# The triangular inverse of a chunked recurrence: moving 32 instead of 64 columns at each level, with a row mask in the addition

## The chip, the cores and the metric

The kernel runs on one core of one Trainium2 chip, everything in fp32. The metric is the device time of one execution in microseconds (us). The kernel before was timed three times.

## What is computed

The program is a whole two-block model: x goes through a Fourier-mixing layer and a recurrent layer (each followed by a mixture of experts) and then through two layers of a second block. The change is in the recurrent layer only, in its scan over time, of which there are two, one forward and one backward:

```python
def wkv_scan(r, decay, k, v, a_vec, b_vec, s0, reverse):
    def step(s, inp):
        r_t, w_t, k_t, v_t, a_t, b_t = inp
        sa = jnp.einsum('bhvk,bhk->bhv', s, a_t)
        s = s * w_t[:, :, None, :] + sa[..., None] * b_t[:, :, None, :] + v_t[..., None] * k_t[:, :, None, :]
        return s, jnp.einsum('bhvk,bhk->bhv', s, r_t)
```

There are 16 heads of 64 values; the scan first goes over 256 context positions (their outputs are not needed), then over 512 image positions.

## The kernel before, in words

The scan is cut into chunks of 64 positions (CH): 4 chunks of context and 8 of the image, 12 steps. In each step (`units`) two units are done together, one of each direction; unit u has its tiles in `scr` for direction 0 and in `ring` for direction 1. Within a chunk the recurrence is solved by a 64x64 triangular inverse for each of the 16 heads. Heads are packed in pairs on the 128 partitions: head 2j on rows 0 to 63, head 2j + 1 on rows 64 to 127 (`rows(q)`), so the tiles XI (the inverse built so far), XT (its transpose), GT and the masks' products NM have 128 rows and 8 x 64 columns.

The inverse is built in LEVELS = 6 doublings. Level 0 is the identity plus the neighbours' entries (L1411). At levels l = 1 to 5 blocks of 2^l are joined to blocks of 2^(l+1), by XI = XI + XI N_l XI, where N_l holds only the entries that join two neighbouring blocks:

1. PE, G (L1479): for each head, NM[l] (64x64) as weights, XT as the moving side, 64 columns. The eight matmuls of a group g of four j are one PSUM bank; two groups per unit. An fp32 matmul is two records in the trace, so a unit's G at one level is 32 records, and both units' 64.
2. ACT (L1329): copies G to GT, 256 columns for each group.
3. PE, P (L1490): GT as weights, XI as the moving side, 64 columns; again 32 records for a unit.
4. DVE (L1421): XI = P + XI, 256 columns per group; then (L1426, not at level 5) two transposes of 256 columns make the new XT, for which G of the next level waits.

The order on PE within a level is G(scr), G(ring), P(scr), P(ring). After P of level 1 come 16 transposes of v (V, L1498), which ACT copies out in eight pieces (L1334) before it copies G of level 2; after P of level 2 come 32 transposes (T, L1504). On DVE a level is four operations for scr, then four for ring; at levels 3 to 5 work for the next step (L1375, L1385 to L1391) is queued between them. Before level 1, ACT copies the product of the step's operands (PE, L1467) out of PSUM and POOL multiplies it with the level masks (L1285), two multiplications of some 1.3 us for each level; G of a level waits for its own. After level 5 PE goes on with Q (L1518, L1519), the output (L1528, L1546), S (L1537) and the state (L1557), and ACT and DVE with their copies.

All engines' orders are written out by hand; semaphores stand only where a value is needed. `pairs`, `each` and `rows` are the helpers for the shapes; MD is a table with two 64-column masks for each direction, loaded once by ACT's DMA (L1303) at the start of the scan.

Of the kernel before, what the change touches and what calls it, by code (L numbers as in the profile page):

```python
# [25 lines left out]
P = 128  # L26
# [13 lines left out]
LEVELS = 6  # L40
# [95 lines left out]
def build(nc, a, out, table):  # L136
# [3 lines left out]
    with ctx:  # L140
# [1093 lines left out]
        BKT = [take_scr(NE, CH), held(2, 1024, NE, CH)]  # L1234
        SV = [take_scr(NE, CH), held(4, 0, NE, CH)]
        ZS = [take_scr(8, CH) for _ in range(2)]
        MD = take_scr(2, 128)
        LM = take_scr(2, LEVELS * CH)
        RST = take_scr(512)
        PT = take_scr(4, 8)  # L1240
# [21 lines left out]

        def pairs(t):
            return t[:, 0:256].rearrange("p (j c) -> p j c", c=CH)

        def chunk_streams(d, img):

# [24 lines left out]
        def wkv_scalar(act):  # L1292
# [19 lines left out]
            for n, pair in enumerate(steps):  # L1312
                for u, d, c, img, first in pair:
                    for b4 in range(4):
                        t = tile(act, f"A{u}.{b4}").rearrange("p (h c) -> p h c", c=128)
                        g, q = divmod(b4, 2)
                        if n and later(act, f"nm{u - 2}.{LEVELS - 1}"):
                            act.wait_ge(*at(f"nm{u - 2}.{LEVELS - 1}"))
                        did(A_, act.activation(odd(SC[d][rows(1 - q), 8 * g:8 * g + 8, :], 1)[:, :, 0:CH],
                                               t[rows(1 - q), :, 0:CH], ACT.Copy).then_inc(scalar_done, 1))  # L1320
                        did(A_, act.activation(odd(SC[d][rows(q), 8 * g:8 * g + 8, :], 0)[:, :, 0:CH],  # L1321
                                               t[rows(q), :, 0:CH], ACT.Copy).then_inc(scalar_done, 1), f"nb{u}.{b4}")
                        if not img:
                            marks[f"free.A{u}.{b4}"] = (A_, count[A_])
                for l in range(1, LEVELS):
                    for u, d, c, img, first in pair:
                        for g in range(2):
                            t = tile(act, f"G{u}.{l}.{g}")
                            did(A_, act.activation(GT[d][:, 4 * g:4 * g + 4, :], pairs(t), ACT.Copy).then_inc(scalar_done, 1), f"free.G{u}.{l}.{g}")  # L1329
                    for u, d, c, img, first in pair if l == 1 else ():  # L1330
                        for g in range(2):
                            t = tile(act, f"V{u}.{g}")[0:64, :].rearrange("p (j q c) -> p j q c", q=2, c=CH)
                            for q in range(2):
                                did(A_, act.activation(odd(SV[d][rows(q), 8 * g:8 * g + 8, :], q), t[:, :, q, :], ACT.Copy).then_inc(scalar_done, 1))  # L1334
                            marks[f"free.V{u}.{g}"] = (A_, count[A_])
                    for u, d, c, img, first in pair if l == 2 else ():
                        for q in range(2):
                            t = tile(act, f"T{u}.{q}")
                            did(A_, act.activation(odd(BKT[d], q), t.rearrange("p (h c) -> p h c", c=CH), ACT.Copy).then_inc(scalar_done, 1), f"free.T{u}.{q}")
                    if n + 1 < len(steps) and l >= 4:  # L1340
                        exps(*steps[n + 1][l - 4])
                for u, d, c, img, first in pair:
                    for g in range(2):
                        t = tile(act, f"Q{u}.{g}")
                        did(A_, act.activation(QB[d][:, 4 * g:4 * g + 4, :], pairs(t), ACT.Copy).then_inc(scalar_done, 1), f"free.Q{u}.{g}")
                for u, d, c, img, first in pair:
                    for g in range(2):
                        t = pairs(tile(act, f"S{u}.{g}"))
                        for q in range(2):
                            did(A_, act.activation(odd(SV[d][rows(1 - q), 8 * g:8 * g + 8, :], q), t[rows(1 - q)], ACT.Copy).then_inc(scalar_done, 1))  # L1350
                        marks[f"free.S{u}.{g}"] = (A_, count[A_])

        def wkv_vector(dve):
# [44 lines left out]
            for n, pair in enumerate(steps):  # L1398
# [17 lines left out]
                for l in range(1, LEVELS):  # L1416
                    for u, d, c, img, first in pair:
                        for g in range(2):
                            t = pairs(tile(dve, f"P{u}.{l}.{g}"))
                            x = XI[d][:, 4 * g:4 * g + 4, :]  # L1420
                            did(V, dve.tensor_tensor(x, t, x, ALU.add).then_inc(vector_done, 1), f"xi{u}.{l}.{g}")  # L1421
                            marks[f"free.P{u}.{l}.{g}"] = (V, count[V])
                        if l < LEVELS - 1:
                            dve.wait_ge(*own(dve, V))
                            for g in range(2):
                                did(V, dve.transpose(flat(XT[d][:, 4 * g:4 * g + 4, :]),  # L1426
                                                     flat(XI[d][:, 4 * g:4 * g + 4, :])).then_inc(vector_done, 1), f"xt{u}.{l}.{g}")
                    if n + 1 < len(steps):
                        if l >= 4:
                            tildes(*steps[n + 1][l - 4])  # L1430
                        if l in (3, 4):
                            scan(*steps[n + 1][l - 3])
# [17 lines left out]
        def wkv_tensor(pe):  # L1450
            def each(g):

                return [(j, q, slice((j % 4) * CH, (j % 4) * CH + CH)) for j in range(4 * g, 4 * g + 4) for q in range(2)]

            for pair in units():
                for u, d, c, img, first in pair:
                    bk, ar = BK[d], AR[(u // 2) % 2][d]
# [12 lines left out]
                for l in range(1, LEVELS):  # L1470
                    for u, d, c, img, first in pair:
                        if later(pe, f"nm{u}.{l}"):
                            pe.wait_ge(*at(f"nm{u}.{l}"))
                        for g in range(2):
                            b = bank(pe, f"G{u}.{l}.{g}")
                            if later(pe, f"xt{u}.{l - 1}.{g}"):
                                pe.wait_ge(*at(f"xt{u}.{l - 1}.{g}"))
                            for j, q, o in each(g):
                                ins = pe.matmul(b[rows(q), o], NM[d][l][rows(q), j, :], XT[d][rows(q), j, :],  # L1479
                                                start=True, stop=True)  # L1480
                            did(T_, ins.then_inc(tensor_done, 1), f"G{u}.{l}.{g}")
                    for u, d, c, img, first in pair:
                        for g in range(2):
                            b = bank(pe, f"P{u}.{l}.{g}")
                            if later(pe, f"free.G{u}.{l}.{g}"):
                                pe.wait_ge(*at(f"free.G{u}.{l}.{g}"))
                            if later(pe, f"xi{u}.{l - 1}.{g}"):
                                pe.wait_ge(*at(f"xi{u}.{l - 1}.{g}"))
                            for j, q, o in each(g):
                                ins = pe.matmul(b[rows(q), o], GT[d][rows(q), j, :], XI[d][rows(q), j, :],  # L1490
                                                start=True, stop=True)
                            did(T_, ins.then_inc(tensor_done, 1), f"P{u}.{l}.{g}")
                    for u, d, c, img, first in pair if l == 1 else ():
                        for g in range(2):
                            b = bank(pe, f"V{u}.{g}")
                            for j in range(4):
                                o = (4 * g + j) * CH
                                ins = pe.transpose(b[0:64, j * P:j * P + P], LD[:, d, 1, o:o + CH], ident[:, :])  # L1498
                            did(T_, ins.then_inc(tensor_done, 1), f"V{u}.{g}")
                    for u, d, c, img, first in pair if l == 2 else ():  # L1500
                        for q in range(2):
                            b = bank(pe, f"T{u}.{q}")
                            for j in range(8):
                                ins = pe.transpose(b[:, j * CH:j * CH + CH], BK[d][rows(q), j, :, :], ident[rows(q), rows(q)])  # L1504
                            did(T_, ins.then_inc(tensor_done, 1), f"T{u}.{q}")
# [1195 lines left out]
def constants():  # L2701
# [22 lines left out]
    md, lm = [], []  # L2724
    for d in range(2):
        strict, incl = (s < t, s <= t) if d == 0 else (s > t, s >= t)
        md.append(np.tile(np.concatenate([strict, incl], 1), (2, 1)))
        for l in range(LEVELS):
            lo, hi = (s >> l, t >> l) if d == 0 else (t >> l, s >> l)
            lm.append(np.tile((lo % 2 == 0) & (hi == lo + 1), (2, 1)))  # L2730
# [74 lines left out]
```

## Time and profile before

| | us |
|---|---|
| median of 3 runs | 4351.8 |
| lowest and highest | 4349.01 and 4355.48 |
| the profiled execution, its own time | 4349.7 |
| its span, first to last instruction | 4347.9 |
| mean granted clock of TensorE in the span | 0.933 |
| matmul busy time (PE) | 3772.8 (87%) |
| VectorE, ScalarE, GpSimd busy | 1400.4, 1036.2, 270.1 |
| the scan, from its first level-1 matmul to its end | 559 (1498.2 to 2057.3 us) |

The profile names instructions by line of the kernel. PE is TensorE's matmuls, PEld its weight loads (which overlap the matmuls), DVE is VectorE, ACT ScalarE, POOL GpSimd. The busy time of PE is a union of overlapping matmuls whose ends are modelled, so the time that a run of matmuls takes is read from start to start. In the rows "64*64" is the part of the array that a matmul uses (rows * columns), "64x64" the moving side (partitions x elements). PEclk is the clock that was granted to TensorE as a share of full speed: 1.0 is 2.4 GHz and 0.5 is 1.2 GHz.

### The profile page before, as it was taken

What the parts mean: (1) busy time and instruction counts of PE and PEld (TensorE: products, weight loads), DVE (VectorE), ACT (ScalarE), POOL (GpSimd) and SP (SyncE); (2) the same over time, 40 slices, a digit from 0 to 9 for tenths busy, and PEclk for the clock granted to TensorE, in tenths of its full rate; (3) what the DMA queues carried; (4) which work ended last, traced back from release to release, by engine and by line L of the source; (5) the groups of instructions that cost most, each with busy time, mean ns of one, the idle gap of its engine ahead of it and who ended that gap; (6) DMA issues with size and microseconds to landing.
All of it is one profiled execution on the core that took longest, in us unless ns stands there. A gap on an engine that the chain in (4) does not pass through costs nothing.

```text
span 4347.9 us, 63440 instructions
## 1 busy us (share of the span) xinstructions
PE 3772.8 (87%) x28402; PEld 2309.3 (53%) x28402; DVE 1400.4 (32%) x2400; ACT 1036.2 (24%) x2049; POOL 270.1 (6%) x248
## 2 busy tenths in 40 slices
PE   7989999999789788888787787789689998968998
PEld 3556344334345488887353232335358874535886
DVE  2123000001562256666320000244433334344343
ACT  3021110111341254444210001123122322212231
POOL 0000000000000234333100000000000000000000
PEclk9988999999799899999989999989799999979999
DMA  8345988992233423322349999411023221102320
GB/s 284 104 148 184 347 307 310 364 337 99 87 118 119 119 51 68 83 62 75 132 175 376 385 376 387 147 60 48 27 68 97 93 71 60 55 30 68 97 88 29
DMA packets 526735, 666.87 MB, mean 153 GB/s; under 512 B 156168, under 2 KB 294664, under 8 KB 526464
## 3 DMA queue, kind: packets, MB, share of 16 engines
q1 hardware_dynamic: 505040, 627.89, 42.4%
q10 hardware_dynamic: 17808, 22.29, 1.6%
q0 software_dynamic: 3616, 12.65, 0.8%
q8 instruction: 223, 3.65, 0.3%
q14 instruction: 48, 0.39, 0.0%
HBM read 631.31 MB, written 31.46 MB: 152 GB/s over the span
## 4 chain that ended last, share of the span: by engine, by line
PE 73%; DVE 9%; ACT 5%; DMA 5%; SPq 4%; issue 1%; POOL 1%; ACTq 1%; DVEq 0%; POOLq 0%
PE ps L604 11%; PE ps L467 8%; PE ps L609 4%; DMA ring<-in_moe_wu 4%; SPq L2497 4%; PE ps L797 3%; PE ps L2362 3%; PE ps L2363 3%; PE ps L2364 3%; PE ps L2378 3%; PE ps L2379 3%; PE ps L2377 3%; PE ps L770 3%; PE ps L2086 3%; PE ps L1479 2%; PE ps L1490 2%
## 5 line engine op out<-in xcount | busy, mean ns | idle before, releaser
L604 PE MATMUL ps<-ring,H 128*64 128x512 f32 x2048 | 494.8, 601 | 52.1 <-DMA ring<-in_moe_wu 39.2
L706 DVE TENSOR_TENSOR scr<-ps,scr 128x512 f32<-128x512 f32 x32 | 22.1, 691 | 965.6 <-PE ps L609 516.9
L604 PEld LDWEIGHTS ps<-ring,H 128*64 128x64 f32 x2048 | 148.4, 137 | 342.5 <-issue 251.2
L604 PE MATMUL ps<-ring,scr 128*64 128x512 f32 x1024 | 248.2, 599 | 39.9 <-DMA ring<-in_moe_wd 38.5
L467 PE MATMUL ps<-scr,ring 128*128 128x512 f32 (+1 forms) x640 | 255.8, 563 | 26.9 <-DVE scr L2312 20.9
L2362 PE MATMUL ps<-scr_rounded,ring_rounded 128*128 128x512 f32 x512 | 203.9, 398 | 29.7 <-ACT scr_rounded L2400 29.7
L2431 DVE TENSOR_TENSOR ring_rounded<-ring,scr_rounded 128x2048 fp32r<-128x2048 f32 x64 | 146.7, 2292 | 227.6 <-ACT scr_rounded L2397 227.6
L467 PEld LDWEIGHTS ps<-scr,ring 128*128 128x128 f32 x640 | 124.0, 195 | 160.0 <-issue 130.7
L2363 PE MATMUL ps<-H_rounded,scr_rounded 128*128 128x512 f32 x512 | 204.0, 398 | 0.0
L2364 PE MATMUL ps<-scr_rounded 128*128 128x512 f32 x512 | 203.8, 398 | 0.0
L2379 PE MATMUL ps<-scr_rounded 128*128 128x512 f32 x512 | 202.5, 395 | 0.0
L2377 PE MATMUL ps<-scr_rounded,ring_rounded 128*128 128x512 f32 x512 | 201.8, 394 | 0.0
L2397 ACT ACTIVATE scr_rounded<-ring 128x2048 fp32r<-128x2048 f32 x64 | 122.1, 1907 | 264.3 <-PE ps L2379 246.4
L604 PEld LDWEIGHTS ps<-ring,scr 128*64 128x64 f32 x1024 | 73.0, 136 | 188.7 <-issue 125.1
L1479 PE MATMUL ps<-scr 64*64 64x64 f32 x1920 | 79.8, 239 | 61.0 <-POOL scr L1285 55.0
L797 PE MATMUL ps<-scr 128*128 128x512 f32 (+1 forms) x320 | 125.9, 556 | 4.2 <-ACT scr L680 2.9
L2362 PEld LDWEIGHTS ps<-scr_rounded,ring_rounded 128*128 128x128 f32 x512 | 97.2, 190 | 55.3 <-DVE H_rounded L2436 31.3
L770 PE MATMUL ps<-scr 128*128 128x256 f32 x512 | 121.5, 390 | 4.0 <-DVE scr L877 4.0
L609 PE MATMUL ps<-ring,H 128*32 128x256 f32 x2048 | 123.8, 382 | 0.0
L1285 POOL TENSOR_TENSOR scr<-scr 128x512 f32<-128x512 f32 x72 | 95.0, 1320 | 332.3 <-ACT scr L1321 332.3
L318 ACT ACTIVATE H<-X 128x512 f32<-128x512 f32 (+1 forms) x56 | 36.5, 659 | 326.9 <-DVE X L485 167.7
L2086 PE MATMUL ps<-H,ring 128*128 128x512 f32 x256 | 110.4, 593 | 3.0 <-DVE scr L2039 3.0
(401 smaller groups left out, 6206.8 us busy)
## 6 DMA issues: line engine op xcount, KB each, us to landing
ring<-in_moe_wg SPq DMA_DIRECT2D x128, 1024.0 KB, 9.5
ring<-in_moe_wu SPq DMA_DIRECT2D x128, 1024.0 KB, 8.7
ring<-in_moe_wd SPq DMA_DIRECT2D x128, 1024.0 KB, 10.1
ring<-in_mlp_w SPq DMA_DIRECT2D x64, 1024.0 KB, 5.3
ring<-in_ada_w SPq DMA_DIRECT2D x48, 1024.0 KB, 7.6
ring<-in_w_in SPq DMA_DIRECT2D x14, 1024.0 KB, 5.2
ring<-in_w_out SPq DMA_DIRECT2D x8, 1024.0 KB, 5.1
st_kka<-scr ACTq DMA_DIRECT2D x16, 384.0 KB, 3.5
```

Of the source, the lines that this page charges most:

```text
L467: ins = pe.matmul(b[:, 0:sn], w[:, k, (m % 2) * P:(m % 2) * P + P], rhs(k, s0, sn), start=k == 0, stop=k == kt - 1)
L604: ins = pe.matmul(bx[64 * n:64 * n + 64, :], stat_x(k), w[:, k % 4, :], start=k == 0, stop=k == KT - 1)
L609: ins = pe.matmul(bc[32 * n:32 * n + 32, 0:256], stat_c(k), w[:, k % 4, o:o + 256], start=k == 0, stop=k == KT - 1)
L770: ins = pe.matmul(b[:, 0:256], HT[:, tt, k * P:k * P + P], GM[:, tt, :], start=tt == 0, stop=tt == 3)
L797: ins = pe.matmul(b[:, 0:sn], ys[:, j, m * P:m * P + P], sm[:, j, :], start=j == 0, stop=j == nj - 1)
L2086: ins = pe.matmul(b, w[:, k, (m % 2) * P:(m % 2) * P + P], H[:, k, 0:TX], start=k == 0, stop=k == KT - 1)
L2362: pe.matmul(b, low[:, k, o], hh, start=k == 0, stop=False)
L2363: pe.matmul(b, high[:, k, o], hl, start=False, stop=False)
L2364: ins = pe.matmul(b, high[:, k, o], hh, start=False, stop=k == KT - 1)
L2377: pe.matmul(banks[m], low[:, k, o], hh, start=f == 0, stop=False)
L2379: ins = pe.matmul(banks[m], high[:, k, o], hh, start=False, stop=f == 15)
L2497: did(f"slot{i % NSLOT}", sp.dma_start(dst, src.rearrange("(k p) c -> p k c", p=min(P, rows))).then_inc(sems[f"slot{i % NSLOT}"], 16), "w. ...
```

## The change

At level l the product XI N_l XI has entries only where a row belongs to a block of one parity and a column to a block of the other. The change moves only the columns of that parity: 32 of 64, as 32 / 2^l blocks of 2^l.

- G streams 32 columns of XT (`half_of(XT, ..., d)`) in place of 64, P 32 columns of XI (`half_of(XI, ..., 1 - d)`). The weights of both are the same 64x64 as before, and the number of matmuls, their order, their banks and all waits too.
- ACT's copy takes 128 columns in place of 256 and writes them in blocks into every second block of GT. The other blocks of GT keep what an earlier level or step left there; the rows of P that come of them are not meant to count.
- DVE's addition takes 128 columns in place of 256, reads and writes XI in blocks, and multiplies P by a column of MD (a value per row, 1 for the rows of the right parity and 0 for the others) first: a scalar_tensor_tensor with a scalar operand in SBUF in the place of a tensor_tensor.
- MD gets six columns more for each direction, its one load too.
- The transposes of XI stay at 256 columns. No instruction is added, removed or moved on any queue.

```diff
@@ -1234,7 +1234,7 @@
-        MD = take_scr(2, 128)
+        MD = take_scr(2, 128 + LEVELS)
@@ -1262,6 +1262,13 @@
+        def blocks(t, l, n):
+
+            return t.rearrange("p j (b two s) -> p j b two s", two=2, s=2 ** l)[:, :, :, n, :]
+
+        def half_pairs(t, l):
+            return t[:, 0:128].rearrange("p (j b s) -> p j b s", j=4, s=2 ** l)
@@ -1326,7 +1333,7 @@
                             t = tile(act, f"G{u}.{l}.{g}")
-                            did(A_, act.activation(GT[d][:, 4 * g:4 * g + 4, :], pairs(t), ACT.Copy).then_inc(scalar_done, 1), f"free.G{u}.{l}.{g}")
+                            did(A_, act.activation(blocks(GT[d][:, 4 * g:4 * g + 4, :], l, d), half_pairs(t, l), ACT.Copy).then_inc(scalar_done, 1), f"free.G{u}.{l}.{g}")
@@ -1416,9 +1423,9 @@
-                            t = pairs(tile(dve, f"P{u}.{l}.{g}"))
-                            x = XI[d][:, 4 * g:4 * g + 4, :]
-                            did(V, dve.tensor_tensor(x, t, x, ALU.add).then_inc(vector_done, 1), f"xi{u}.{l}.{g}")
+                            t = half_pairs(tile(dve, f"P{u}.{l}.{g}"), l)
+                            x = blocks(XI[d][:, 4 * g:4 * g + 4, :], l, 1 - d)
+                            did(V, dve.scalar_tensor_tensor(x, t, MD[:, d, 128 + l:129 + l], x, ALU.mult, ALU.add).then_inc(vector_done, 1), f"xi{u}.{l}.{g}")
@@ -1452,6 +1459,12 @@
+            def each_half(g):
+                return [(j, q, slice((j % 4) * 32, (j % 4) * 32 + 32)) for j in range(4 * g, 4 * g + 4) for q in range(2)]
+
+            def half_of(t, q, j, l, n):
+                return t[rows(q), j, :].rearrange("p (b two s) -> p b two s", two=2, s=2 ** l)[:, :, n, :]
@@ -1475,8 +1488,8 @@
-                            for j, q, o in each(g):
-                                ins = pe.matmul(b[rows(q), o], NM[d][l][rows(q), j, :], XT[d][rows(q), j, :],
+                            for j, q, o in each_half(g):
+                                ins = pe.matmul(b[rows(q), o], NM[d][l][rows(q), j, :], half_of(XT[d], q, j, l, d),
                                                 start=True, stop=True)
@@ -1486,8 +1499,8 @@
-                            for j, q, o in each(g):
-                                ins = pe.matmul(b[rows(q), o], GT[d][rows(q), j, :], XI[d][rows(q), j, :],
+                            for j, q, o in each_half(g):
+                                ins = pe.matmul(b[rows(q), o], GT[d][rows(q), j, :], half_of(XI[d], q, j, l, 1 - d),
                                                 start=True, stop=True)
@@ -2724,7 +2737,8 @@
-        md.append(np.tile(np.concatenate([strict, incl], 1), (2, 1)))
+        even = [(np.arange(64)[:, None] >> l) % 2 == d for l in range(LEVELS)]
+        md.append(np.tile(np.concatenate([strict, incl] + even, 1), (2, 1)))
```


## Rows read from the trace of the kernel before

**Rows 1.** The page's part 4, the chain that ended last by engine.

```profile
PE 73%; DVE 9%; ACT 5%; DMA 5%; SPq 4%; issue 1%; POOL 1%; ACTq 1%; DVEq 0%; POOLq 0%
```

**Rows 2.** Busy time by stretch: us, PE, PEld, DVE, ACT, POOL, PEclk, DMA share, GB/s. Scan; level 1's matmuls; after.

```profile
1498.20:2057.30 559.10, 484.95 (x13056) 465.95 (x13056) 355.44 (x770) 280.53 (x748) 212.42 (x165) 0.94 0.30 68
1775.80:1779.10 3.30, 3.30 (x64) 3.30 (x66) 1.15 (x2) 1.15 (x3) 3.30 (x3) 0.51 0.00 0
1779.20:1802.80 23.60, 22.30 (x653) 21.37 (x651) 16.60 (x39) 11.99 (x31) 10.47 (x9) 1.00 0.62 136
```

**Rows 3.** Chain that ended last, 1440 to 2090 us: start us, us, what.

```profile
1501.88 2.24 PE ps L1490 x64
...
1774.02 1.68 POOL scr L1285
1775.74 3.57 PE ps L1479 x64
1779.31 1.87 PE ps L1490 x64
...
2021.54 1.86 PE ps L1490 x64
```

**Rows 4.** Timeline of one step, 1779 to 1801 us: start us, us, engine, line, op, tiles, xcount [idle before].

```profile
1781.11 1.94 PE L1498 MATMUL ps<-ident,H 128*64 128x128 f32 x16
...
1785.50 1.15 PE L1490 MATMUL ps<-scr 64*64 64x64 f32 x32 [0.45 <-ACT scr L1329]
...
1790.99 1.10 PE L1490 MATMUL ps<-scr 64*64 64x64 f32 x32
...
1794.04 0.77 DVE L1426 STREAM_TRANSPOSE ring<-ring 128x256 f32<-128x256 f32 x2
...
1794.63 1.15 PE L1479 MATMUL ps<-ring 64*64 64x64 f32 x32 [0.30 <-DVE ring L1426]
...
1795.59 1.13 PE L1490 MATMUL ps<-scr 64*64 64x64 f32 x32
...
1800.20 1.01 PE L1490 MATMUL ps<-scr 64*64 64x64 f32 x28
```

**Rows 5.** Durations by line (ns min/median/max): level matmuls' weight loads, and L410's.

```profile
L1490 PEld LDWEIGHTS ps<-scr x1920: 129/135/224, 1501.6 to 2044.0; 64*64 64x64 f32 x192
...
L410 PEld LDWEIGHTS ps<-vec,scr x192: 186/192/338, 22.8 to 364.8; 128*128 128x128 f32 x192
```

**Rows 6.** Timeline of PE at 351 us, line 410 at the full clock.

```profile
351.55 0.61 PE L410 MATMUL ps<-vec,scr 128*128 128x2 f32 x4
```

**Rows 7.** Groups by form, whole span: xcount | busy us, mean ns | idle before.

```profile
L706 DVE TENSOR_TENSOR scr<-ps,scr 128x512 f32<-128x512 f32 x32 | 22.1, 691 | 965.6 <-PE ps L609 516.9 <-PE ps L604 448.7
...
L487 DVE SCALAR_TENSOR_TENSOR X<-ps,ada,X 128x256 f32<-128x256 f32 x16 | 7.7, 484 | 29.0 <-PE ps L467 21.6 <-PE ps L797 7.5
...
L1883 ACT ACTIVATE scr<-ps 128x128 f32<-128x128 f32 x12 | 3.3, 277 | 6.9 <-PE ps L1816 6.9
```

**Rows 8.** Groups by form, 1440 to 2080 us, the lines that the change touches.

```profile
L1490 PE MATMUL ps<-scr 64*64 64x64 f32 x1920 | 71.5, 226 | 5.8 <-ACT scr L1329 5.4 <-issue 0.4
...
L1421 DVE TENSOR_TENSOR scr<-ps,scr 128x256 f32<-128x256 f32 x120 | 49.6, 421 | 115.4 <-PE ps L1490 113.4
...
L1329 ACT ACTIVATE scr<-ps 128x256 f32<-128x256 f32 x120 | 43.8, 391 | 105.6 <-PE ps L1479 103.4
```

**Rows 9.** Timeline of PE: matmuls of 64 rows, of 6 rows, then of 128 rows.

```profile
1137.66 21.26 PE L958 MATMUL ps<-scr,ring 64*128 64x512 f32 x32 [1.83 <-ACT scr L1125]
...
3070.14 10.57 PE L2097 MATMUL ps<-H 6*128 6x512 f32 x12 [8.62 <-DVE H L2229]
...
3081.40 1.97 PE L2109 MATMUL ps<-ident,scr 128*128 128x128 f32 x8
```

**Rows 10.** Busy time by stretch, columns as in rows 2: the first two of rows 9.

```profile
1137.40:1157.80 20.40, 20.08 (x30) 10.01 (x31) 6.19 (x11) 11.27 (x22) 3.59 (x6) 0.50 0.65 250
3070.20:3080.60 10.40, 10.40 (x14) 4.04 (x14) 0.00 (x0) 2.98 (x5) 0.00 (x0) 0.50 0.00 0
```


## The prediction

> **What bounds the kernel now.** I first read the chain of waits for the whole span: 73% of it is PE and 9% DVE [rows 1], so time comes off where PE works or waits for DVE. The scan takes 559.1 us of the 4347.9 [rows 2]; nothing outside it is touched. Then the chain inside the scan [rows 3]. A step begins when POOL has made the masks' products, and the next rows are all PE: the 64 records of G at level 1 take 3.57 us, those of P 1.87 us. The same kind of matmul at two speeds: 56 ns a record, then 29. The rows of stretches [rows 2] say why: over the first the granted clock is 0.51 (1.2 GHz), over everything from P to the end of level 5 it is 1.00 (2.4 GHz). The clock has fallen while PE waited for POOL, and it comes back in the middle of level 1, after about one G. The twelve P rows of level 1 run from 2.24 us (first) to 1.86 (last), mean 2.16 [rows 3]: the clock is back for most of each.
>
> The timeline of one step [rows 4] shows the rest. Level 1 ends in V at 1781.11. At level 2 P(scr) waits 0.45 us for ACT, which is still copying V; such waits are 5.4 us in all, 0.45 for each of the 12 steps [rows 8]. At levels 3 to 5 P(scr) starts at 1790.99, 1795.59 and 1800.20, every 4.6 us, while four groups of 0.93 us are 3.7 us. The rest is DVE: G(ring) waits 0.30 us for the transpose that began at 1794.04. So two intervals of a step hang on a loop PE, DVE, PE; the others are PE's own pace.
>
> **The change, part by part.**
>
> *PE's pace at 2.4 GHz: no change.* 32 moving columns in place of 64 halve what is streamed. The question is whether the stream sets the 29 ns a record. Line 410 streams 2 columns against weights of 128 columns: four records in 0.61 us, of which the last one's own 0.251 is latency, so 0.12 us each [rows 6]. Two columns cannot cost that; the weight load does. A load of 128 columns lasts 186 ns at the least, one of 64 columns 129 [rows 5]: 57 ns for 64 columns. The level's matmuls use two corners of the array at once (head 2j, head 2j + 1), so 57 ns of loading on each corner is 28.5 ns a record, what we see. The weights stay 64 columns, hence 0. Bounds: 0, and a halving to 15 ns a record if the stream set the pace (a rival below); I take 0, since [rows 5, 6] are about the load itself. The Trainium skill (TensorE: Matmul & The Clock Gate, LDWEIGHTS) says that a load takes its columns / 1.2 ns, whatever the rows: 53 ns here; the trace agrees. Its section on the back-to-back issue gap has a floor of about 25 ns start to start however few columns are streamed; by it alone a group would go from 0.93 to 0.80 us, and the 20 groups of a step would give back at most 2.6 us. The two-column matmuls [rows 6] speak for the load.
>
> *The clock at level 1: it comes back later.* What raised it was G of level 1. In 1.2 GHz a pair of records takes 115 ns (2 x 57.5), and each corner streams in 107 of them (64 columns at two cycles each), nearly without pause. That the clock does not look at matmuls in flight alone is shown elsewhere [rows 9, 10]: matmuls of 64 rows run for 21.26 us, and of 6 rows for 10.57 us, back to back, PE busy throughout, and the clock stays at 0.50 for the whole time. After the change each corner streams in 53 of 115 ns, so G of level 1 comes to look like those 64-row matmuls rather than like G of today. I therefore expect G and P of level 1 to pass at 1.2 GHz, and the clock to rise in V, 16 transposes with all 128 rows and 128 moving columns. Costs per step: P takes 64 x 57.5 ns = 3.68 us for a mean of 2.16, **+1.5**. V takes at 1.2 GHz 16 x 0.22 = 3.5 us (eight of that shape are 1.97 us including latency [rows 9]) for 1.94, so between 0 and +1.6; since G needed its 3.6 us to raise the clock, I take **+1.3**.
>
> *ACT.* 128 elements of PSUM cost 277 ns, 256 cost 391 [rows 7, 8]: -0.11 us each. Only one copy is on the path, that which P(scr) of level 2 awaits. With V slower, ACT's copies of V finish behind it and well before G of level 2 has run, so the whole wait goes: **-0.45**. At the least it is -0.11.
>
> *DVE.* An addition of 256 elements takes 421 ns and one of 512 takes 691 [rows 7, 8]: 1.05 ns an element, so 128 fewer save 0.13 us. But the scalar operand costs: a scalar_tensor_tensor with one, PSUM and SBUF, takes 484 ns at 256 [rows 7], 0.06 more. Net -0.07 us, 350 ns an addition. In the loop lie the second addition of scr and both of ring (their start-to-start is the part that counts, and it shrinks by less, 0.04 for the first), so about -0.19 us, with -0.03 for P's last record ending 27 ns sooner: -0.215 a loop, two loops a step, **-0.4**. Bounds: 0, if pieces of 2 to 32 elements cost DVE what they save, and -0.4 a loop if the scalar costs nothing. At the other levels DVE is not waited for.
>
> *Free.* MD's load has 12 columns more of 268, once. The transposes, POOL's work, all waits and all orders are the same. If POOL's cover went, G of a level would wait for its mask; it is made levels ahead except at level 1, where POOL, not PE, sets the start, before and after.
>
> Sum per step: 1.5 + 1.3 - 0.45 - 0.4 = +1.95 us, times 12 = **+23 us**. Against the profiled execution's own 4349.7 (span 4347.9 and 1.8 around it) that is 4373; the median of the runs is 2.1 higher, so I predict **4375 us**, 0.5% slower.
>
> **The rivals.**
>
> *A, the above: the clock is late at level 1 and holds afterwards.* 0.55.
>
> *B, it also falls again inside the levels.* At levels 3 to 5 PE will stream half of what it does now, with the gap of the DVE loop still there. Where the clock falls a level of 128 records takes 128 x 57.5 = 7.4 us for 4.6, 2.8 more, or 8.3 us a step until Q (64 columns again) raises it. In every other step that is +50, so 4425; in all steps +100, 4475. For: the stream is as thin as in [rows 9]. Against: now PE pauses in every level too [rows 4], and the clock holds [rows 2]. 0.15.
>
> *C, the clock comes back as before.* The clock would then follow the loads and matmuls as such, of which there are as many as before. Only the gains stand: 12 x (0.43 + 0.11) = -6.5, so 4345, and no measurable difference. Against: [rows 10]. This is also the case in which the change does not do what it says, since PE's work shrinks on paper alone. 0.18.
>
> *D, the other side: the stream sets PE's pace.* The place is every G and P; the price 14.6 ns a record at 2.4 GHz, 28.8 at 1.2. G of level 1 saves 1.8 us, P of level 1 0.9, level 2 1.9 less 0.9 of longer waiting for ACT; each of the two loops holds two groups of 0.47 less and DVE's 0.2, 2.3 together, and the last two groups save 0.9: some 7 us a step, 84 in all, 4268. It decides if a record falls below 29 ns in the timeline. For: two streams of 64 columns are 53 ns on a corner, close to 58, so the present pace can't tell the two apart. Against: [rows 5, 6]. 0.12.
>
> **How the numbers follow.** A measurement of this kernel tells 0.2%, 8.7 us, from no change. A and B are slower: 0.70. C is within it for 0.14, and with a cheaper DVE operand beyond it for 0.04; with D, faster has 0.16. The range goes from C's time, 4343, to B's with half of the steps, 4430; outside it are D and the worse half of B, 0.19. A's own range is 4360 (V's term 0) to 4385.
>
> **What would show it.** In the changed kernel's timeline: 32 records of G or P at 2.4 GHz still in 0.93 us from start to start (if 0.5: D). In the stretches from the start of G at level 1: clock 0.5 through P, and P's 64 records 3.7 us in the chain, not 1.9 (if 1.9: C). V in 3 us or more. No wait of P at level 2 for ACT. P(scr) of levels 3, 4, 5 every 4.4 us with the clock at 1.0; 7.4 and 0.5 would be B. L1421's successor at 350 ns and ACT's copy at 277. The prediction is wrong if the scan, 559 us now, is shorter than 555 or longer than 635.

## The result, and the profile after

| | before | after |
|---|---|---|
| median of 4 runs, us | 4353.34 | 4425.72 |
| lowest and highest | 4349.01 and 4355.48 | 4417.92 and 4431.71 |
| ratio of the times | | 1.0167, interval 1.0144 to 1.0189 |
| profiled execution: span, us | 4347.9 | 4429.9 |
| mean granted clock | 0.933 | 0.908 |

The change makes the kernel 72 us slower, where 23 were forecast. The scan's stretches of time in the kernel after (columns as in [rows 2]; the scan as a whole, then one step in three pieces, then most of another step):

```profile
1495.40:2133.80 638.40, 577.69 (x12996) 554.74 (x12998) 339.33 (x765) 262.25 (x748) 209.90 (x165) 0.76 0.27 59
1767.90:1778.50 10.60, 10.57 (x146) 9.57 (x146) 4.06 (x10) 3.41 (x10) 10.60 (x9) 0.50 0.02 6
1778.60:1795.30 16.70, 15.27 (x478) 14.83 (x477) 10.88 (x28) 7.70 (x23) 3.02 (x3) 1.00 0.85 188
1795.60:1802.00 6.40, 6.40 (x133) 6.40 (x132) 5.41 (x12) 1.80 (x4) 0.00 (x0) 0.50 0.01 3
1592.20:1636.00 43.80, 43.77 (x769) 42.58 (x771) 19.91 (x48) 13.49 (x38) 13.74 (x11) 0.51 0.30 62
```

The clock over the scan is 0.76, where it was 0.94 [rows 2]. In the step from 1767.90 it is 0.50 through all of level 1 (G, P and V), then 1.00, and 0.50 again from the last P on. Before, it was 1.00 from P of level 1 to the end of level 5. The step from 1592.20 never gets it back before Q. The chain of waits of the same two steps (start, us, what; lines are those of the kernel after: L1492 is G, L1503 P, L1511 V):

```profile
1592.22 3.62 PE ps L1492 x64
1595.85 3.41 PE ps L1503 x64
1599.26 3.55 PE ps L1511 x16
...
1767.93 3.63 PE ps L1492 x64
1771.56 3.41 PE ps L1503 x64
1774.97 3.55 PE ps L1511 x16
1778.52 2.00 PE ps L1492 x64
1780.52 1.87 PE ps L1503 x64
...
1795.55 2.97 PE ps L1503 x58
```

Against [rows 3]: G of level 1 is as long as before (3.63 for 3.57), P 3.41 for a mean of 2.16, V 3.55 for 1.94 [rows 4]. P at full clock is 1.87 for 64 records, to the digit what it was with 64 columns. The waits of PE in the scan (us in total, times, longest), and the groups by shape (busy us, mean ns):

```profile
PE ps L1492 <- issue: 2.8, 3, 1.1
PE ps L1492 <- DVE ring L1433: 2.3, 12, 0.4
PE ps L1503 <- issue: 0.6, 2, 0.4
```

```profile
L1428 DVE SCALAR_TENSOR_TENSOR scr<-ps,scr 128x128 f32<-128x128 f32 x120 | 41.2, 348 | 170.0 <-PE ps L1503 166.4
L1336 ACT ACTIVATE scr<-ps 128x128 f32<-128x128 f32 x120 | 32.4, 286 | 128.0 <-PE ps L1492 127.9
```

Besides POOL's 54.9 us ahead of level 1, these are all. P's wait for ACT (5.4 us before, [rows 8]) is gone, an addition takes 348 ns and a copy 286.

To see where the 12 steps spend their time, I took from the timeline of PE the starts of A (the step's operand products), of G of each level, and of Q (L1518 before), and summed the distances over the steps. "Q to A" runs to the next step's A, so it has 11 terms; "all" is the whole row, from the first A to the last Q. The same sums of the experiments below stand here, in us:

| kernel | A to G1 | level 1 | level 2 | level 3 | level 4 | level 5 | Q to A | all |
|---|---|---|---|---|---|---|---|---|
| before | 118.0 | 91.0 | 73.2 | 50.1 | 56.0 | 51.2 | 119.5 | 559.0 |
| after | 118.0 | 125.2 | 75.1 | 54.7 | 63.5 | 68.4 | 133.5 | 638.4 |
| w_l1 | 118.1 | 93.1 | 73.5 | 53.9 | 61.9 | 69.0 | 136.0 | 605.4 |
| w_l2up | 118.1 | 124.9 | 69.1 | 49.2 | 56.0 | 49.5 | 119.8 | 586.7 |
| w_l3up | 118.1 | 124.3 | 67.7 | 51.5 | 56.2 | 47.5 | 119.6 | 584.8 |
| w32 | 118.1 | 79.6 | 60.0 | 45.0 | 60.5 | 48.6 | 132.0 | 543.7 |
| half_add | 118.1 | 91.2 | 73.2 | 49.4 | 56.4 | 48.6 | 120.0 | 556.9 |
| before_fill | 120.8 | 77.1 | 73.2 | 50.4 | 55.4 | 49.2 | 117.2 | 543.3 |
| after_fill | 120.8 | 84.8 | 68.9 | 49.0 | 65.6 | 71.6 | 135.1 | 595.7 |
| after_fill_lv | 120.8 | 101.0 | 74.1 | 60.4 | 64.1 | 55.0 | 116.8 | 592.1 |
| after_fill_ld | 120.8 | 91.9 | 73.9 | 80.1 | 99.9 | 90.3 | 130.9 | 687.8 |
| half_add_fill | 121.0 | 77.1 | 73.3 | 49.8 | 51.1 | 50.7 | 118.8 | 541.8 |
| w_all_fill | 120.6 | 77.1 | 72.0 | 49.9 | 53.6 | 49.2 | 120.2 | 542.6 |

Each row is one execution. That of after is the longest of its four (4431.71 us), so its scan is 79 us longer than before's where the medians are 72 apart. The kernel w_all, below, has no row, since its profiled execution ran in a slow state, at a clock of 0.553 (6515.73 us), while its other eleven took 4342.51 to 4349.60 us.

After against before: level 1 costs 34.2 us more, and levels 2 to 5 and the stretch behind Q 45.2 more. The first number is in the prediction. The second isn't.

### The profile page after: what moved, and what is told of

Same layout as the page of the kernel before. It is cut to its first block, busy times and chain, and to the rows that moved or that the text cites. A ratio compares the mean times of both kernels' runs of the same rounds, so it can differ in the third digit from the quotient of the medians.

```text
span 4429.9 us, 63440 instructions
## 1 busy us (share of the span) xinstructions
PE 3866.1 (87%) x28402; PEld 2401.2 (54%) x28402; DVE 1387.3 (31%) x2400; ACT 1017.9 (23%) x2049; POOL 267.5 (6%) x248
## 4 chain that ended last, share of the span: by engine, by line
PE 75%; DVE 9%; DMA 5%; ACT 4%; SPq 4%; issue 1%; POOL 1%; ACTq 1%; DVEq 0%; POOLq 0%
PE ps L604 11%; PE ps L467 8%; DMA ring<-in_moe_wu 4%; PE ps L609 4%; SPq L2510 4%; PE ps L1492 3%; PE ps L1503 3%; PE ps L797 3%; PE ps L2377 3%; PE ps L2375 3%; PE ps L2376 3%; PE ps L2391 3%; PE ps L2392 3%; PE ps L2390 3%; PE ps L770 3%; PE ps L2099 2%
## 5 line engine op out<-in xcount | busy, mean ns | idle before, releaser
L1492 PE MATMUL ps<-scr 64*64 64x32 f32 x1920 | 88.2, 251 | 59.1 <-POOL scr L1292 54.9
L2375 PEld LDWEIGHTS ps<-scr_rounded,ring_rounded 128*128 128x128 f32 x512 | 97.2, 190 | 54.9 <-DVE H_rounded L2449 31.3
L1492 PEld LDWEIGHTS ps<-scr 64*64 64x64 f32 x1920 | 81.6, 172 | 66.7 <-POOL scr L1292 57.1
```

The costliest lines, as they stand in the source:

```text
L1492: ins = pe.matmul(b[rows(q), o], NM[d][l][rows(q), j, :], half_of(XT[d], q, j, l, d), start=True, stop=True)
L2375: pe.matmul(b, low[:, k, o], hh, start=k == 0, stop=False)
```

## The experiments

Theory 1 is that the 34 + 45 us are all clock, the granted clock of TensorE: a stream of 32 columns neither raises a fallen clock (level 1) nor holds a raised one (levels 3 to 5). Against it stand other costs of the change (pieces of few elements on ACT and DVE, the row mask), a single late rise with consequences, and pauses of PE. The first four kernels were timed together with the kernel before, which took 4350.81 us there.

**w_all**: everything as in the change, but PE streams all 64 columns. ACT and DVE take their 128 elements out of PSUM in blocks.

```diff
-                            for j, q, o in each_half(g):
-                                ins = pe.matmul(b[rows(q), o], NM[d][l][rows(q), j, :], half_of(XT[d], q, j, l, d),
+                            for j, q, o in (each(g) if l >= 1 else each_half(g)):
+                                ins = pe.matmul(b[rows(q), o], NM[d][l][rows(q), j, :], XT[d][rows(q), j, :] if l >= 1 else half_of(XT[d], q, j, l, d),
```

(P likewise, and `blocks(pairs(t), ...)` for `half_pairs(t, l)` on ACT and DVE. Every level has l >= 1, so all are wide.)

> The change with TensorE left as it was: G and P stream 64 columns again, while ScalarE's copy and VectorE's masked addition take only the 128 elements that the change takes (read from PSUM in blocks). Theory 1 (the time was lost by TensorE's clock, because fewer columns are streamed): the clock comes back in level 1 and holds, mean granted clock 0.93, and only the gains of the shorter copy and addition are left: 4345 to 4349 us. Theory 2 (the short pieces, the scalar operand or the block pattern cost the time): slower than before by tens of us, near 4425, with additions or copies longer than 350 and 280 ns or a clock that falls all the same.

Measured 4345.69, ratio 0.9987 (0.9978 to 0.9996). The whole loss is in PE's stream; the copy and the masked addition at half width gain some 5 us, between 2 and 10.

**w_l2up** and **w_l1**: 32 columns at level 1 alone, and at levels 2 to 5 alone (`each(g) if l >= 2 else each_half(g)`, and `l == 1`).

> The change at level 1 only: 32 columns streamed by G and P of level 1, 64 at levels 2 to 5; the copy and the addition at 128 elements everywhere. Theory 1: level 1 takes 10.3 us a step as in the change (7.6 before), so +33, the rest as before less some 6: about 4379 us. If the loss of the levels 3 to 5 and of Q were carried over from a late level 1, the time stays near 4425.

> The change at levels 2 to 5 only: 64 columns streamed at level 1, 32 at levels 2 to 5; copy and addition at 128 elements everywhere. Theory 1: the clock comes back in level 1 (7.6 us a step), then falls again at level 4 or 5 in most steps; no step stays at 1.2 GHz from level 1 to Q, as two do in the change, so about 4380 us (4370 to 4395). If instead the late rise at level 1 is the cause of the later falls, the clock holds and the time is 4345 to 4350.

Measured 4376.99, ratio 1.0057 (1.0043 to 1.0071), and 4396.42, ratio 1.0099 (1.0086 to 1.0113). The chain at level 1, first of w_l2up (L1493 is G, L1504 P):

```profile
1787.04 3.63 PE ps L1493 x64
1790.67 3.41 PE ps L1504 x64
...
1797.51 2.01 PE ps L1493 x64
```

then of w_l1, with the last P of the step:

```profile
1746.09 3.68 PE ps L1493 x64
1749.77 2.47 PE ps L1504 x64
...
1771.14 2.73 PE ps L1504 x58
```

w_l2up has level 1 of the kernel after (124.9 us) and, behind it, everything of before. In w_l1 the clock comes back within level 1 (93.1 us), yet the clock falls in its levels 3 to 5 and behind Q as it does after (69.0 at level 5 and 136.0 behind Q). The two losses, 26 and 46 us, make 72 together: two costs, each with its own place, and the second doesn't follow from the first. w_l1 came out just above the expected 4395, since the clock fell earlier than I had priced: in one step (the second) before level 3, in another within it.

**w32**: the changed kernel with 32 weight columns as well, so half of each product is left out.

```diff
-                                ins = pe.matmul(b[rows(q), o], NM[d][l][rows(q), j, :], half_of(XT[d], q, j, l, d),
+                                ins = pe.matmul(b[64 * q:64 * q + 32, o], NM[d][l][rows(q), j, 0:32], half_of(XT[d], q, j, l, d),
```

(P likewise. ACT's copy is scaled by 1e-6, and DVE's mask column is another column of MD.)

> G and P with weights of 32 columns and 32 streamed columns. Left out: half of each product, and GT is scaled down to nearly nothing, so XI stays at level 0's value; every instruction is there. If the load of 64 weight columns sets the 58 ns of a pair of records, a pair now takes about 30 ns at 2.4 GHz (32 records in 0.48 us) and the level's streams fill that again, so that the clock comes back in level 1 as before: about 4270 us (4260 to 4290). If a fixed cost of an instruction sets it (25 ns or more), 32 records take 0.8 us or stay at 0.93, and the clock behaves as in the change: 4400 or more.

Measured 4336.36, ratio 0.9962 (0.9947 to 0.9977). PE's timeline:

```profile
1774.42 0.69 PE L1492 MATMUL ps<-scr 64*32 64x32 f32 x32
1774.94 0.68 PE L1492 MATMUL ps<-ring 64*32 64x32 f32 x32
...
1787.52 0.51 PE L1492 MATMUL ps<-scr 64*32 64x32 f32 x21 [1.51 <-DVE scr L1433]
```

32 records now take 0.52 us from start to start, 16 ns each, with the same 32 moving columns that took 29 with 64 weight columns. So it is the weight columns, and with them the load, that set the pace at full clock, as the prediction had it. The clock in level 1 of the same step, G and P, then V, and the longest waits of PE in the scan besides POOL's:

```profile
1768.20:1772.50 4.30, 3.69 (x128) 3.54 (x128) 2.18 (x5) 1.15 (x4) 4.30 (x4) 0.50 0.02 4
1772.60:1774.40 1.80, 1.80 (x18) 1.62 (x16) 1.63 (x6) 1.13 (x3) 1.80 (x2) 1.00 0.00 0
```

```profile
PE ps L1503 <- issue: 15.6, 11, 2.7
PE ps L1492 <- issue: 14.9, 17, 1.9
PE ps L1503 <- ACT scr L1336: 14.8, 18, 1.2
PE ps L1492 <- DVE scr L1433: 8.4, 16, 1.5
```

With loads and streams both halved, the stream is as dense in time as before, and the clock does return inside level 1 (79.6 us in all). But in this step it returns only as V begins, so w32 doesn't separate what the dense stream of G and P does for the rise from what V does. The time missed the expected 4270 because PE, done sooner, now stops more: it waits for DVE (1.51 us in the timeline above) and for ACT, and for 30.5 us in G and P with nothing that the profile shows as its reason ("issue"), where the kernel before had 4.1. That pause is the largest of these and its cause isn't known. The clock falls in levels 4 and 5 and behind Q (60.5, 48.6, 132.0); that it falls for these stops wasn't tested. The Trainium skill (TensorE: Matmul & The Clock Gate, Back-to-back issue gap) gives an issue floor of about 25 ns a matmul for 1 to 64 moving columns. Two matmuls on different corners of the array don't keep to it: 16 ns in the mean here.

The next four kernels, half_add_fill at the end among them, were timed with the kernel before at 4349.06 us.

**half_add**: the kernel before with DVE's addition alone at half width, from P in blocks, without a mask.

```diff
-                            t = pairs(tile(dve, f"P{u}.{l}.{g}"))
-                            x = XI[d][:, 4 * g:4 * g + 4, :]
+                            t = blocks(pairs(tile(dve, f"P{u}.{l}.{g}")), l, 1 - d)
+                            x = blocks(XI[d][:, 4 * g:4 * g + 4, :], l, 1 - d)
```

> The kernel before, with one edit: DVE's addition takes only the 128 elements of the right parity, in blocks, out of P as it stands (64 columns, so no row is wrong and no mask is needed: a tensor_tensor without a scalar operand). PE, ACT and the clock's work are untouched. Theory 1 (DVE's part of the change is worth its terms, and only the stream of PE costs): an addition takes 0.29 us in place of 0.42; the two loops of a step that hang on DVE give back 0.25 to 0.4 us each, 12 steps, so -6 to -10 us: 4341 to 4345 for 4350.8, ratio 0.998 to 0.9986. Rival (pieces of 2 elements cost DVE what it saves, or the loop isn't DVE's): 4350, ratio 1.000.

Measured 4347.95, ratio 0.9995 (0.9987 to 1.0004): no difference that can be told, though the loop did shorten. PE's waits, a row of the timeline and the stretch around it:

```profile
PE ps L1482 <- issue: 4.2, 7, 0.9
PE ps L1493 <- issue: 4.1, 5, 1.2
```

```profile
1790.74 0.50 PE L1482 MATMUL ps<-scr 64*64 64x64 f32 x10 [0.67 <-issue]
```

```profile
1790.00:1790.90 0.90, 0.23 (x8) 0.15 (x6) 0.90 (x3) 0.36 (x1) 0.00 (x0) 1.00 0.51 113
```

In five of the steps level 4 takes 4.21 or 4.22 us in place of 4.62. In others PE stops in the middle of a G or P, for up to 1.2 us, again for "issue": 8.3 us in G and P, where the kernel before had 4.1. That takes back most of the gain. What PE waits for there isn't known; I didn't test it. The pause is also a first word on the clock: it stays at 1.00 across 0.67 us without work, between levels that stream 64 columns.

**before_fill**: the kernel before with five matmuls of 512 columns on PE while POOL makes the first mask's products. They write the bank that G of level 1 then overwrites. PE's wait for the mask moves behind them.

```diff
                             b = bank(pe, f"G{u}.{l}.{g}")
+                            if l == 1 and d == 0 and g == 0:
+                                for _ in range(5):
+                                    pe.matmul(b[:, 0:512], ident[:, :], FILL, start=True, stop=True)
```

> The kernel before with five matmuls of 128x128 weights and 512 moving columns queued on PE ahead of level 1, whose result is overwritten by G: PE works on nothing useful while POOL makes the first mask's products. Theory 1 (what the clock falls for is the missing stream of PE in that wait, and level 1 then pays for it): the clock is 1.0 when G of level 1 begins, G's 64 records take 1.9 us in place of 3.6, P's 1.9 in place of a mean of 2.2: -2.0 us a step, less up to 0.4 where the filler ends behind POOL: -19 to -24 us, 4327 to 4332, ratio 0.995 to 0.9957. Rival (the clock falls in each step for another reason, or is given back late whatever PE does): G of level 1 at 3.6 us and the time at 4350 or, with the filler in the way, up to 4360.

Measured 4333.45, ratio 0.9966 (0.9952 to 0.9979). PE's timeline from the filler on, and the stretch from G of level 1 to the end of level 5:

```profile
1760.84 4.56 PE L1479 MATMUL ps<-scr,ident 128*128 128x512 f32 x10
1765.63 1.15 PE L1485 MATMUL ps<-scr 64*64 64x64 f32 x32 [0.23 <-POOL scr L1285]
1767.31 1.15 PE L1485 MATMUL ps<-ring 64*64 64x64 f32 x32 [0.53 <-POOL ring L1285]
```

```profile
1765.60:1791.00 25.40, 23.47 (x681) 22.40 (x683) 16.88 (x41) 13.14 (x34) 13.95 (x11) 1.00 0.59 128
```

The clock is 1.00 throughout and level 1 takes 6.49 us in nearly every step (mean 7.58 before). The gain is 16 us and not 19 to 24, because the stall that goes uncovers the next: G(ring) now waits 0.53 us for its own mask, which POOL makes after that of scr. At half clock G(scr) had hidden it.

**after_fill**: the same filler in the changed kernel.

> The changed kernel with the same five filler matmuls ahead of level 1. Theory 1 (the change costs +34 us in level 1 because thin streams don't raise a fallen clock, and +44 later because they don't hold it): with the clock up at level 1's start its 64 records of G take 1.9 us; if the clock held through, all of the change's loss would go and 4325 would come out. It won't quite: falls inside levels 3 to 5 stay in most steps, and there may be some at level 1 or 2 now. So -34 - 20 of 4424: 4360 to 4385, ratio 1.002 to 1.008. Rival 1 (one late rise is the whole cause and the later falls follow from it): 4325 to 4335. Rival 2 (thin streams let a raised clock fall at once): G and P of level 1 at 1.2 GHz again, 4400 to 4430.

Measured 4395.14, ratio 1.0111 (1.0094 to 1.0129). By the ratios the filler is worth 0.34% (15 us) to the kernel before and 0.56% (24 us) to the changed one (1.0167 to 1.0111), and a loss of 62 us against before_fill stays. PE's timeline in level 4 of one step (L1498 is G, L1509 P) and at V of level 1 of the next (L1517):

```profile
1758.61 1.33 PE L1498 MATMUL ps<-ring 64*64 64x32 f32 x32 [0.17 <-DVE ring L1433]
1759.68 1.96 PE L1509 MATMUL ps<-scr 64*64 64x32 f32 x32
...
1797.78 3.15 PE L1517 MATMUL ps<-ident,H 128*64 128x128 f32 x16
```

Rival 1, the one late rise, is out: with the clock up at level 1's start, levels 4 and 5 and the stretch behind Q still take 272.3 us, where before has 226.7 and after 265.4. Of Rival 2 there is some truth: G and P of level 1 begin at full clock, but in five of the steps it is lost before V ends (level 1 takes about 8.05 there, not 6.46), though PE doesn't wait for DVE inside level 1. That is why the time lies above the expected 4385.

The last four kernels (the next two, w_l3up and w_all_fill) were timed with the kernel before at 4352.94 us.

**after_fill_lv** and **after_fill_ld**: after_fill, with filler in PE's pauses of levels 3 to 5 too: 128 moving columns in the first, 2 in the second, with the same 128x128 weights.

```diff
+                            if l >= 3 and g == 0:
+                                for _ in range(1 + d):
+                                    pe.matmul(b[:, 0:128], ident[:, :], FILL[:, 0:128], start=True, stop=True)
```

(`0:2` in both places for the second.)

> The changed kernel with the five filler matmuls ahead of level 1, and at levels 3 to 5 with filler inside the levels: one matmul of 128x128 weights and 128 moving columns where PE waits for DVE's transpose before G of scr, two before G of ring (about 0.24 us each, beside pauses of 0.1 to 0.6 us). Theory 1 (the later falls come of the thin stream in the levels): the clock holds at 1.0 through levels 3 to 5 and Q; level 4, level 5 and the stretch after Q go back from 65.6, 71.6 and 135.1 us (after_fill) to about 55, 52 and 120, with up to 10 us for the filler itself: 4345 to 4360, ratio 0.999 to 1.003. Rival (the fall has another reason, for instance Q's or the copies' pauses): after_fill's 4395 or, with the filler in the way, 4400 to 4410.

> The control to after_fill_lv: the same filler matmuls in levels 3 to 5 with the same 128x128 weights, but 2 moving columns in place of 128 (the five ahead of level 1 stay as they are). A weight load of 128 columns sets the pace of either, so PE is as long busy in the pauses and loads as much; only the columns that are streamed are missing. Theory 1 (what counts is the stream, not the pause): the clock falls in levels 3 to 5 as in after_fill, 4390 to 4405, ratio 1.010 to 1.013. Rival (a pause in PE's work, whatever it streams, is what lets the clock fall): as after_fill_lv, 4345 to 4360.

Measured 4384.48, ratio 1.0085 (1.0054 to 1.0115), and 4484.35, ratio 1.0304 (1.029 to 1.0318). A level of after_fill_lv (L1495 is the filler, L1501 G) and the stretch over its levels 2 to 5:

```profile
1757.27 0.71 PE L1495 MATMUL ps<-scr,ident 128*128 128x128 f32 x4
1757.92 1.12 PE L1501 MATMUL ps<-ring 64*64 64x32 f32 x32
```

```profile
1796.80:1818.00 21.20, 21.20 (x596) 20.16 (x597) 13.38 (x34) 8.57 (x25) 4.14 (x4) 1.00 0.69 150
```

The same of after_fill_ld, in level 4 and over levels 4 and 5; then, in an earlier step, the stretch from the first filler of level 3 to where the clock falls, and from there to the end of level 5:

```profile
1797.50 1.01 PE L1495 MATMUL ps<-scr,ident 128*128 128x2 f32 x4
1798.44 1.92 PE L1501 MATMUL ps<-ring 64*64 64x32 f32 x32
```

```profile
1795.20:1812.00 16.80, 16.80 (x271) 16.54 (x274) 9.70 (x21) 4.29 (x12) 0.00 (x0) 0.50 0.35 71
1565.60:1568.10 2.50, 2.50 (x61) 2.43 (x60) 0.06 (x1) 1.69 (x5) 1.29 (x2) 1.00 0.42 81
1568.30:1589.00 20.70, 20.70 (x342) 20.38 (x342) 10.78 (x25) 4.74 (x14) 0.00 (x0) 0.50 0.28 63
```

These two settle the later falls. PE is busy without a pause in these stretches; the loads are the same, the number of matmuls too. With 128 columns in the filler the clock is 1.00 through levels 3 to 5 and Q in 11 of 12 steps (level 4 at 5.03 us). With 2 columns it is 0.50 (level 4 at 8.57 us in 11 of 12 steps), and it falls earlier than without any filler: level 3 takes 80.1 us over the steps, where after_fill had 49.0. In the last two rows it falls between 1568.1 and 1568.3, in level 3, and PE hasn't paused in that level. So the pauses of levels 3 to 5 aren't needed for the fall. Filling a pause with loads doesn't hold the clock, filling it with a stream does. The fillers read their columns in one piece, so it is their number that counts here and not the pattern of blocks in which the change reads its columns. The Trainium skill (TensorE: Matmul & The Clock Gate, HAM oscillation) explains such falls by stretches in which the engine waits between bursts of matmuls and advises to order the loop so that it stays busy; by that the second kernel should have held. The measurement speaks against it as a rule for thin matmuls.

Both times missed what I had written. In after_fill_lv the filler costs about 20 us (levels 3 and 4 take 5.03 where G and P with DVE's loop need 4.01 and 4.37), twice my figure, and the clock is lost in level 1 in 9 of 12 steps, where after_fill lost it in five (101.0 us for 84.8). In after_fill_ld I had taken after_fill's falls as they were; they became more.

**w_l3up**: 32 columns at levels 1 and 2 (`l >= 3` wide).

> 32 columns at levels 1 and 2, 64 at levels 3 to 5. Theory 1: level 1 pays +34 us as in the changed kernel and with 64 columns at levels 2 to 5 (4376 there); level 2 has no wait for DVE, so its 32 columns are followed by 32 transposes of T and by wide levels, and a fall is either absent or made up for; in one or two steps the clock may come back later. 4375 to 4390, ratio 1.0055 to 1.009. Rival (thin streams at level 2 cost as much as at levels 3 to 5): over 4395.

Measured 4378.17, ratio 1.0064 (1.0048 to 1.0079), as expected and as w_l2up (1.0057): behind a thin level 1, whose clock rises late, a thin level 2 costs nothing. Of the 46 us of w_l1 nearly all is paid from level 3 on. Whether its thin level 2 helps to bring on those falls isn't shown: no run has 32 columns at levels 3 to 5 alone, and in one step of w_l1 the clock falls inside level 2.

**half_add_fill** and **w_all_fill**: the filler ahead of level 1 with half_add, and with w_all.

> Both together on the kernel before: the half addition, PE's streams of 64 columns kept, and the five filler matmuls ahead of level 1. The gains lie in different places (level 1, and the loops of levels 3 to 5), so they should add: -8 and -21 us, 4318 to 4326, ratio 0.9925 to 0.9945. Rival (DVE becomes faster in a place where PE then runs at a fallen clock, or the filler makes levels 3 to 5 wait for something else): the better of the two alone, about 4330.

> The parts of the change that gained something, with what holds the clock: PE streams 64 columns at all levels as before, ACT's copy and DVE's masked addition take 128 elements, and five filler matmuls stand ahead of level 1. Theory 1: before_fill's -16 to -19 us, and what w_all gained (-2 to -5): 4328 to 4332, ratio 0.995 to 0.996; within 2 us of half_add_fill. Level 4 at 4.3 to 4.4 us a step and G of level 1 at 1.9 us. Rival (the half-width copy and addition make PE wait for its instructions more, so nothing is left of their gain): 4333 to 4335, as before_fill.

Measured 4330.24, ratio 0.9963 (0.995 to 0.9975), and 4331.88, ratio 0.9954 (0.9941 to 0.9966). Two levels of half_add_fill in the chain, then the wait of its PE that has grown:

```profile
2015.77 1.15 PE ps L1488 x32
...
2019.99 1.15 PE ps L1488 x32
```

```profile
PE ps L1499 <- issue: 4.7, 7, 1.5
```

The loop is 4.22 us, 0.4 less than before_fill's, but the "issue" pauses (0.8 us there) have grown with it. half_add_fill missed its expected 4318 to 4326 and can't be told from before_fill; w_all_fill came as expected. So the versions that beat both kernels do so by the filler, 0.3 to 0.5% against before and some 2% against the change. What the change's copy and addition add to before_fill (0.9966) is within the intervals.

## Why the prediction was wrong

**PE's pace** (no change): right. 64 records of P take 1.87 us with 32 columns and with 64; w32 shows the load as the reason. Rival D is out.

**The clock at level 1** (+2.8 a step, 33.6 in all): right in place and sum, 34.2 measured, and the sum partly by luck, since its terms were off in opposite ways. P costs +1.25 and not +1.5. I had used 57.5 ns a record, a G of 3.68 us in the chain over its 64 records; but such a piece has the slow first records and the end of the last one in it. The starts of the groups, here with 64 columns in the kernel before, are 1.70 us apart for 32 records:

```profile
1874.42 1.92 PE L1479 MATMUL ps<-ring 64*64 64x64 f32 x32
1876.12 1.92 PE L1490 MATMUL ps<-scr 64*64 64x64 f32 x32
1877.83 0.84 PE L1490 MATMUL ps<-ring 64*64 64x64 f32 x20
```

That is 53 ns a record at half clock, the same as with 32 columns (3.41 us for 64). V costs +1.6 and not +1.3, the upper bound, and in two steps V doesn't raise the clock at all: all of their levels run at half clock. Rival C is out.

**ACT** (-0.45): right, the wait is gone. Level 2 takes 5.41 us in the good steps for 6.10.

**DVE** (-0.4 for two loops): right to the trace, 4.37 us a loop for 4.6, an addition 348 ns against a forecast of 350. But half_add shows only 1 us of it in the kernel's time (its interval goes from 6 us gained to 2 lost); by its trace the "issue" pauses eat most. The sum had no place for them.

**The step that failed** is "A, the above: the clock is late at level 1 and holds afterwards", in the sum a zero for the clock at levels 2 to 5 and behind Q. There the kernel after takes 45.2 of its 79 us more. w_l2up, whose clock holds there, takes 6.4 less than before in the same columns, so the falls cost about 52 us (an estimate from the table). I had the rival (B) and gave it 0.15 with the words "Against: now PE pauses in every level too [rows 4], and the clock holds [rows 2]." That reasoning took the pauses as the danger and their survival as the evidence. after_fill_lv and after_fill_ld show that what counts is how much is streamed, with pauses or without, and the change halved exactly that. [Rows 9] already had PE at work without any pause and a clock that stayed down, with matmuls of few rows; I used it for the rise and not for the hold.

B named the mechanism but not its size. 4425 was "every other step", 2.8 us a level from level 3 on. In truth 9 of the 12 steps fall, in level 4 or 5, two stay at half clock from level 1 to Q, and one holds; a level at half clock takes 6.83 us for 4.62 (level 4), 2.2 more, since a record takes 53 ns and not 57.5; and the stretch behind Q, which B's price left out, pays 14 us.

That the time came out at 4425.7, B's number, is therefore luck. It lies within the range of 4343 to 4430; the side was right, the size a third of what was measured.

## What to carry to other kernels

Before you halve the moving columns of small matmuls, ask what sets their pace. If it is the weight load, the records don't follow each other any faster, and the stream gets thinner in time, which can cost the clock twice: where it has to be raised after a wait, and where it has to be held afterwards. Take the two as separate terms, and for each compare columns streamed per time, and the rows that they use, with a stretch of the same trace where the clock did or didn't hold ([rows 9] had many columns on few rows and stayed at 0.50). Where PE must wait anyway, wide matmuls into a bank that is about to be overwritten are a cheap way to keep it up (here 16 us); but look at what is next in line behind the wait.

## What the runs showed of the hardware

- The clock isn't held by weight loads and matmul instructions as such: levels of back-to-back matmuls with 32 and 2 moving columns ran at 0.50 (after_fill_ld), with 32 and 128 at 1.00 (after_fill_lv).
- fp32 matmuls of 64 rows on two corners of the array: 29 ns a record with 64 weight columns, whether 64 or 32 are moved (1.87 us for 64 records, before and after); 16 ns with 32 and 32 (w32). At half clock a record is 53 ns, again whether 64 or 32 are moved (1.70 us for 32 before, 3.41 for 64 after).
- A scalar_tensor_tensor with a scalar operand and blocks of 2 to 32 elements takes 348 ns for 128 elements of PSUM in the mean (after); 350 had been worked out from instructions without blocks.
- Shortening PE's or DVE's part of a level brought out pauses in which PE waits for nothing that the profile shows: up to 1.5 us (half_add_fill) and 2.7 us (w32), 30.5 us in all in w32 for 4.1 before. Their cause is open.
